# A fused two-block model on one core: front and both ends of the recurrence rebuilt, one inverse turned on VectorE, modulation products spread out

## What is computed

```python
m_lat = silu(c) @ mod_w + mod_b          # six rows of 1024; the same for c_ctx
h_ctx = rmsnorm(ctx, norm1_pre) * (1 + m_ctx[1]) + m_ctx[0]     # 256 tokens
h     = rmsnorm(x, norm1_pre) * (1 + m_lat[1]) + m_lat[0]       # 512 tokens
cols  = h @ w_in                         # hyena, rwkv and gate columns
kk = heads(k * k_k); kk = kk * rsqrt(max(sum(kk * kk), 1e-24))  # 8 heads of 64
for each of two directions:              # recurrence over 256 + 512 tokens
    S = S * w_t + (S @ a_t) b_t + v_t k_t ;  y = S @ r_t
y = head_groupnorm(y_0 + y_1) * ln_g + ln_b + bonus ;  y = y * (sigmoid(lg) @ g_up)
```

## Time and profile before

| | us |
|---|---|
| median of 3 runs (4183.6 to 4188.72) | 4186.31 |
| the profiled execution's own time | 4191.89 |
| its span | 4190.1 |
| PE busy | 3504.0 (84%) |
| VectorE busy | 1176.1 (28%) |
| ScalarE busy | 608.9 (15%) |
| mean DMA rate | 159 GB/s |

### The profile page before, as it was taken

The page is one execution under the profiler, slowest core; times in us unless marked ns, Lnnn a source line. Parts: engine busy times, 40 slices in busy tenths (PEclk is TensorE's granted clock), DMA queues, the critical chain, the costliest instruction groups (busy, mean ns, idle before and its releaser), DMA issues. The chain is left out here.

```text
span 4190.1 us, 50871 instructions
## 1 busy us (share of the span) xinstructions
PE 3504.0 (84%) x22440; PEld 1717.7 (41%) x22440; DVE 1176.1 (28%) x1979; ACT 608.9 (15%) x1182; POOL 7.9 (0%) x36
## 2 busy tenths in 40 slices
PE   3777899766989787777777789998999995999999
PEld 1446787632433432222222224345444443444443
DVE  0244556533200400000000002475366304122210
ACT  0113223111000210000000002215211102121100
POOL 0000000000000000000000000000000000000000
PEclk7888999877999699999999999999999996999999
DMA  9023322301012139999999971110243325312211
GB/s 334 21 66 124 123 84 89 80 30 64 31 60 75 42 158 421 422 420 421 422 418 421 421 311 44 61 51 16 71 148 116 113 71 155 106 60 80 80 66 50
DMA packets 227200, 664.82 MB, mean 159 GB/s; under 512 B 36960, under 2 KB 101156, under 8 KB 176293
## 3 DMA queue, kind: packets, MB, share of 16 engines
q1 hardware_dynamic: 225224, 661.02, 41.5%
q10 hardware_dynamic: 1757, 0.56, 0.1%
HBM read 638.84 MB, written 20.21 MB: 157 GB/s over the span
## 5 line engine op out<-in xcount | busy, mean ns | idle before, releaser
L2386 PE MATMUL banks<-h_T,weight_ring 128*128 128x512 f32 x1408 | 614.3, 597 | 5.8 <-PEq L89 5.8
L1820 PE MATMUL banks<-weight_ring,xe_T 128*64 128x512 f32 x2048 | 470.4, 602 | 150.1 <-DMA weight_ring<-in_exp_w 148.0
L2386 PEld LDWEIGHTS banks<-h_T,weight_ring 128*128 128x128 f32 x1408 | 268.0, 192 | 338.8 <-issue 338.7
L1820 PEld LDWEIGHTS banks<-weight_ring,xe_T 128*64 128x64 f32 x2048 | 143.2, 137 | 466.8 <-issue 260.0
L1600 PE MATMUL banks<-weight_ring,ffn_act 128*128 128x512 f32 x704 | 307.3, 600 | 14.5 <-PEq L2536 7.5
L1835 PE MATMUL banks<-weight_ring,hid_T 128*64 128x512 f32 x1024 | 235.3, 602 | 83.4 <-DMA weight_ring<-in_exp_w 82.5
L2445 DVE SCALAR_TENSOR_TENSOR conv<-banks,cols,conv 128x510 f32<-128x510 f32 (+1 forms) x176 | 131.9, 749 | 342.5 <-ACT conv L2415 337.8
L1600 PEld LDWEIGHTS banks<-weight_ring,ffn_act 128*128 128x128 f32 x704 | 135.4, 193 | 186.4 <-issue 186.4
L1889 DVE TENSOR_TENSOR hid<-silu,banks 128x1024 f32<-128x1024 f32 x16 | 19.5, 1221 | 665.8 <-issue 570.7
L549 PE MATMUL banks<-h_T,weight_ring 128*128 128x512 f32 x416 | 180.5, 592 | 3.2 <-PEq L89 3.2
L1835 PEld LDWEIGHTS banks<-weight_ring,hid_T 128*64 128x64 f32 x1024 | 71.4, 137 | 246.6 <-issue 142.2
(11 more groups left out here) (541 smaller groups left out, 3929.5 us busy)
## 6 DMA issues: line engine op xcount, KB each, us to landing
weight_ring<-in_exp_w SPq DMA_DIRECT2D x192, 2048.0 KB, 11.2
weight_ring<-in_ada_w SPq DMA_DIRECT2D x24, 2048.0 KB, 10.3
weight_ring<-in_ffn_w_up SPq DMA_DIRECT2D x44, 1024.0 KB, 7.5
weight_ring<-in_mod_w SPq DMA_DIRECT2D x12, 2048.0 KB, 9.0
weight_ring<-in_ffn_w_down SPq DMA_DIRECT2D x10, 2048.0 KB, 7.8
weight_ring<-in_attn_w_in SPq DMA_DIRECT2D x7, 2048.0 KB, 7.8
weight_ring<-in_w_in SPq DMA_DIRECT2D x6, 2048.0 KB, 9.8
weight_ring<-in_w_in SPq DMA_DIRECT2D x9, 1024.0 KB, 7.8
```

What stands on the lines that cost most here:

```text
L1820: mm = pe.matmul(k.ps[64 * half:64 * half + 64, 2 * c + b % 2, :], xeT[:, kt, e * CAP:(e + 1) * CAP], w[:, r, 512 * b:512 * b + 512], star ...
L2386: mm = pe.matmul(k.ps[:, b + c, :], w[:, c, kt, m * P:m * P + P], hT[:, kt, :], start=kt == 0, stop=kt == 7)
```

## The change

Only the first block's mixer and the order of its weights change.

- `modulation` and `small_columns` go. `front` does the first four chunks of mod_w (shift and scale of the first norm) and the norms of context and x in one stage. The partial sums are added and turned by four matmuls of two columns (`modulation_columns`), with no transfers. x is issued behind the ring's first three chunks, context at the stage's start. h of the 512 tokens is stored to DRAM.
- Chunks 4 to 7 of mod_w go into `rwkv_prepare`, 8 to 11 into `rwkv_finish`.
- `rwkv_prepare` gathers the lengths of all 8 heads on 8 partitions (headsel), has one root, one maximum and one reciprocal of 8x768, and spreads them again by matmuls (pick). `rwkv_finish` does the same with 8x512. It works on four tiles side by side.
- In the scan T is no longer carried by a product of its own: VectorE turns TT into T in 32x32 blocks (the last level, which couples blocks of 32, needs no T). Two of a round's four modulation products stand between the chain's halves, one each behind levels 1 and 3.
- The reload of x and the second `normed_columns` go: h and x are loaded during `rwkv_finish`.

```diff
-    out += [[rows(I["mod_w"][0], 0, 8, 512 * j, 512)] for j in range(12)]
+    out += [[rows(I["mod_w"][0], 0, 8, 512 * j, 512)] for j in range(FRONT_MODS)]
     out += [[rows(w_in, 0, 8, HY_COLS + 512 * j, min(512, RW_COLS - 512 * j))] for j in range(4)]
+    out += [[rows(I["mod_w"][0], 0, 8, 512 * j, 512)] for j in range(FRONT_MODS, FRONT_MODS + LATE_A)]
...
-            sync.dma_start(k.x[:], I["x"][0].rearrange("(t p) n -> p t n", p=P)).then_inc(consts_landed, 16)
             k.ring.load_ahead(sync, 0)
+            sync.dma_start(k.x[:], I["x"][0].rearrange("(t p) n -> p t n", p=P)).then_inc(k.rows_landed, 16)
...
+def modulation_columns(pe, k, part, bank, col0, n):
+
+    for m in range(4):
+        mm = pe.matmul(k.ps[:, bank, col0 + n * m:col0 + n * m + n], part[:, m * P:m * P + P], k.misc[:, 7:7 + n],
+                       start=True, stop=True)
+    return mm
```

The front's TensorE and ScalarE programs:

```diff
+            for j in range(n_chunks):
+                k.ring.wait(pe, j)
+                modulation_product(pe, k, j, j).then_inc(products, 1)
+                if j:
+                    turn_columns(j - 1)
+            turn_columns(n_chunks - 1)
+            pe.wait_ge(normed, tiles)
+            for j in range(DT):
+                a, b = pairs[j % 4]
+                if j == 3:
+                    pe.wait_ge(factors, 1)
+                if j >= 4:
+                    pe.wait_ge(evac_a, j - 3)
+                    pe.wait_ge(evac_v, j - 3)
...
+            for j in range(n_chunks - 1):
+                copy(j)
+            act.wait_ge(k.rows_landed, 32)
+            for u in range(tiles):
+                if u:
+                    act.wait_ge(squares, u)
+                act.activation(sqr[:], source(u), ACT.Square, accum_out=ss[:, 0, u:u + 1]).then_inc(squares, 1)
```

rwkv_prepare and the scan:

```diff
+            product(0)
+            product(1)
+            pe.wait_ge(loads, 96)
+            for j in range(RW_T):
+                pe.wait_ge(squared, j + 1)
+                pe.matmul(k.ps[0:2 * RW_T, 0, :], B.headsel[:, j, :], sqr[:, j % 2, 0:L], start=j == 0, stop=j == RW_T - 1)
...
-                pe.wait_ge(act_done, act_n[("siga", n, 1)])
-                for m in range(4):
-                    k.ring.wait(pe, 4 * n + m)
-                    ev(("mod", 4 * n + m), M.products(pe, k, 4 * n + m, (6, 7, 2, 5)[m]))
+                else:
+                    early_products(0)
...
                         products(("X", n, l, d), n, d, 3 * d + 1, "T", "Y")
-                        if l < LEVELS - 1:
-                            products(("XT", n, l, d), n, d, 3 * d + 2, "Y", "T")
+                    if l % 2:
+                        modulate(4 * n + 2 + l // 2)
...
-                    ev(("T1", n, d), dve.tensor_tensor(masks("T", d), masks("L", d), mask(d, "pair"), ALU.mult))
-                    after(("T1", n, d))
-                    ev(("T", n, d), dve.tensor_tensor(masks("T", d), masks("T", d), eye8, ALU.add))
...
+                    after(("TT", n, d))
+                    ev(("T", n, d), dve.transpose(flat("T", d), flat("TT", d)))
...
+    doubling = (("TTl", 0, 0), ("Tl", 0, 0), ("TTl", 0, 1), ("Y", 1, 0), ("Tl", 0, 1), ("Y", 1, 1))
```

rwkv_finish (SyncE, and the order on TensorE):

```diff
+            sync.dma_start(gup, k.I["rw_g_up"][0]).then_inc(gate_landed, 16)
+            sync.dma_start(k.hT[:], k.h_rows).then_inc(k.h_stored, 16)
+            sync.dma_start(k.x[:], k.I["x"][0].rearrange("(t p) n -> p t n", p=P)).then_inc(k.rows_landed, 16)
+            k.ring.load_ahead(sync, LATE_B)
...
+    pe_n = counted([("mean", 0), ("mean", 1), ("bonus", 0), ("bonus", 1), ("mean", 2), ("mean", 3)] + [("head", j) for j in last] +
+                   [("bonus", 2), ("bonus", 3), ("mod", 0), ("mod", 1), ("gate", 0), ("gate", 1), ("mod", 2), ("share", 0), ("share", 1),
+                    ("mod", 3), ("share", 2), ("gate", 2), ("share", 3), ("gate", 3), "columns"])
```

More of the change, by code:

```diff
@@ L413, in _ @@
             def _(pe):
[L414 to L417, removed]
+                for q in range(4):
+                    mm = pe.matmul(k.ps[:, 0, 0:self.rows], self.tiles[:, q, :], k.sq("eye")[0:self.rows, 0:self.rows],
+                                   start=q == 0, stop=q == 3)
                 mm.then_inc(turned, 1)
@@ L422, in _ @@
                 dve.wait_ge(turned, 1)
[L423 to L452, removed]
-                    if j >= M.n_buf:
-                        act.wait_ge(spread[j % M.n_buf], 64 * M.n * (j // M.n_buf))
-                    act.activation(M.part[:, j % M.n_buf, :], k.ps[:, j % 4, :], ACT.Copy).then_inc(copied, 1)
-                    act.wait_ge(copied, j + 1)
-                    for dma in M.spread(act, j, j % M.n_buf):
-                        dma.then_inc(spread[j % M.n_buf], 16)
-                for b in range(M.n_buf):
-                    act.wait_ge(spread[b], 64 * M.n * (n_chunks // M.n_buf))
-        k.ring.done(n_chunks)
-        M.finish(k, out, bias_name, bias0)
@@ L480, in _, with copy @@
         @block.scalar
         def _(act):
[L482 to L492 removed]
+            def copy(j):
+                act.wait_ge(products, j + 1)
+                act.sem_inc(k.ring.used, 1)
+                act.activation(part[:, j, :], k.ps[:, j, :], ACT.Copy).then_inc(copied, 1)
@@ L847, in _, with copy, values @@
-            act.activation(B.lwla[0:64, :], B.lwla[0:64, :], ACT.Tanh)
-            act.activation(B.lg[:], B.lg[:], ACT.Sigmoid)
-            for c in range(TOK // P):
+            def copy(m):
+                act.wait_ge(products, m + 1)
+                act.sem_inc(k.ring.used, 1)
+                act.activation(part[:, m, :], k.ps[:, 6 + m % 2, :], ACT.Copy).then_inc(copied, 1)
+            def values(c):
                 act.wait_ge(turned, c + 1)
@@ L1024, in chain, with modulate, early_products @@
                         ev(("y", n, i), mm)
+                    if i == 0 and not last:
+                        early_products(n + 1)
+            def modulate(m):
+                k.ring.wait(pe, m)
+                ev(("mod", m), M.products(pe, k, m, MOD_BANK[m % 4]))
+            def early_products(n):
+                pe.wait_ge(act_done, act_n[("siga", n, 1)])
+                for m in range(2):
+                    modulate(4 * n + m)
             def products(name, n, d, bank, left, right):
@@ L1395 @@
+    k.ring.done(LATE_B)
 class RwkvBuffers:
```

554 lines of the change are left out of this document (338 added, 216 removed).

## The result

The changed kernel takes **4007.8 us** (median of 4 runs, 4003.3 to 4015.8) against 4187.3 us before (4 runs): ratio 0.9575, 95% interval 0.9558 to 0.9591. That is 180 us less; 224 were predicted, and 4007.8 lies 2.8 us outside the range. The profiled execution took 4006.8 us with a span of 4005.0, so 185 us less than the 4190.1 of before. (The medians give 5 us less: the profiled execution of before took 4191.9, 4.6 above its median.)

The account below looks back on a forecast made before the run. Outside the projection, PE was taken to wait in the stages ahead of the untouched 3294 us, whose savings reach the end one for one; -83 - 9 - 83 - 49 = -224, against the median 4186.3 gives 3962 us, range 3932 to 4005.

Parts of the forecast that it names:

- Front (-83): Stages ahead of the first projection: four chunks instead of twelve, no spreads; projection starts at 59.5 instead of 142.4, -83 us.
- Transposition (t = 0.69): VectorE's transposition of 128x512 in the scan, taken at 0.69 us like a tensor-tensor of the same size.
- the transposition is dear: Rival, chance 0.13: the scan's VectorE transpositions cost more; 3995 at 1.24 us each, 4102 at 3.35.
- the estimate of 1.24 us: Scan transposition of 512 columns, priced as four times the skill page's 311 ns; +33 us on the sum.
- Scan (-83): Scan rounds: inverse starts 11.3 us earlier and takes 2.8 less, one latent round -14.1, sum -83 us.
- in two of the four level changes a modulation product of 1.79 stands ahead of the next Y: Scan's inverse: 1.55 of each product shows, so levels of 4.2 and 5.75 us, 19.9 for 22.7.
- Behind the scan (-49): rwkv_finish and the stage after it: 26 us go whole, the rest by four tiles together; -49 us, ends -30 and -52.
- the gain's store and the barriers: the next projection at about 846.5: End of the stage behind the scan: VectorE's last column at 842, next projection at about 846.5.
- what would make it wrong: Wrong if inverse levels wait for chunks, PE's clock falls there, or reloading h and x delays chunks behind the scan.
- rwkv_prepare (-9): rwkv_prepare and the Silu stage: scan starts at 305.5 instead of 314.6, -9 us, ends -11 and +13.
- columns 1.2, two shares 2.8: End of PE's chain in rwkv_prepare at full clock: columns 1.2 us, last two shares 2.8, to 302.7.
- Half clock in the moved products: Rival, chance 0.12: rwkv_prepare and the stage behind the scan keep the low clock, +22 and +19, 4003.

Follow-up runs that it names:

- e7: Changed kernel with a second, idle transposition of the same size ahead of each of the 60 in the scan; 4025.4 us.
- e4: Changed kernel with the two chunks per round that the level products set free cut to their first eighth, part of the loading left out; 3987.9 us.
- e3: Changed kernel with the two chunks that the level products set free issued only behind the inverse; 4002.8 us.
- e5: Changed kernel with the level products' chunks loaded in four pieces of 512 KB, each gated by a later event; 3990.6 us.
- e11: Changed kernel with the level products' chunks loaded in two pieces of 1 MB; 3994.6 us.
- e8: e1 with the recurrence's projection loading two chunks ahead, the third issued in rwkv_prepare behind the small loads; 3995.7 us.
- e1: Changed kernel with the six gain stores moved from rwkv_finish to the head of the hyena projection's stage; 3998.0 us.
- e2: Changed kernel with five of the gain stores issued at the head of rwkv_finish, ahead of its loads; 4023.2 us.

## Why the prediction missed by 40 us

- **Front (-83): right.** Measured -83.9, with the first projection product at 58.5 where 59.5 was worked out. The steps came out as well: the root at 43.2 for 43.4, the last normed tile at 47.7 for 47.9.
- **Transposition (t = 0.69): right,** 0.706 to 0.711; levels 4.2 us, and 10.14 for the two of which one holds a product. The rival "the transposition is dear" is out, and with it the estimate of 1.24 us. Its slope was too steep besides: in e7 0.7 us more for each cost 0.29, not 0.7.
- **Scan (-83): the chain was right, and a cost was missing.** The step that failed is "in two of the four level changes a modulation product of 1.79 stands ahead of the next Y", which costed the moved product alone. The product also brings its DMA: the 2 MB transfer that it triggers now runs beside the densest instruction stretches of the program (16 records of a modulation product take 1.8 us, 32 of the inverse 0.94), and PE stops there for want of instructions. Before, the transfers ran beside the modulation products and L and stopped PE for 8.9 us; now it is 17.3, and the pair of levels with one product takes 12.12 us for 9.95 in round 3. With that transfer shrunk, the scan is 409.3 us for a forecast of 409.8. Round 3, which had only 0.7 us of stops before, gains 14.0 for 14.1; that the whole comes so close is in part luck, for e4 also lacks 6.6 us of the stops that the forecast kept. That the transfer's burst causes the stops is shown by e3, e4, e5 and e11. That it does so by delaying instructions is shown by the packets of the instruction queue, late in the burst, with every stop ending just behind one. How the two share the DMA engines, and why PE needs another 2.4 to 2.7 us, no run shows.
- **Behind the scan (-49): mis-sized by 15 us.** The step is "the gain's store and the barriers: the next projection at about 846.5", which gave a few us for the end. PE's and VectorE's work was as reckoned (VectorE's last column 36.3 us behind the turn of the modulation; forecast 34.6, 842 less 807.4). The six stores of 4-byte elements behind three chunks took 25.6 us of SyncE's time. With them elsewhere the tail is 38.7 (e8) to 42.7 us (e1), for 39.1 forecast. The "what would make it wrong" clause looked at the reload of h and x, which held up nothing: the fourth chunk was late by 0.79 us.
- **rwkv_prepare (-9): mis-sized by 6 us.** The step is "columns 1.2, two shares 2.8" with the full clock assumed for them. The columns took 4.2 us, the last two shares 5.5 and the two turns before them 3.3 for 1.9: 7 us more, at a granted clock of 0.63. The 3.6 us wait for the small loads was not reckoned either, but it cost nothing against the forecast, because the first two products took 3.6 us where 7.2 were put: the head sums ended 12.4 us into the stage, for 12.8. e8 shows the same from the other side: its wait is 0.3, its first two products take 5.3, and the stage is only 2.0 us shorter.
- **Half clock in the moved products**: the mean granted clock rose from 0.62 to 0.84 and from 0.60 to 0.76 in these stages, so the rival did not come as priced (+22 and +19). It came in part, in the last 13 us of rwkv_prepare. That its time (4003) was near is chance.
- **The range** took in each rival alone. What happened was two unforeseen collisions in the DMA system at once, in the two stages that lack 37 us together, in a kernel whose steps were all costed on PE, ACT and VectorE.

## What to carry to other kernels

When an instruction that frees a buffer is moved, move its transfer along in your mind: ask what runs beside that burst. A large prefetch does not only compete for bytes; cut into pieces of 0.5 to 1 MB that are gated by progress, it cost this PE-dense loop 4 to 5 us where whole chunks cost 17.

A stage that ends in a barrier ends with its last issue too: look at the queue ahead of the final stores, and put stores of 4-byte elements where neither a load nor a barrier stands behind them.

## What the runs showed of the hardware

- PE's instructions come in packets of 16 KB, one for every 254 to 257 records (82 in the scan of the changed kernel, 93 before). Where a packet came late beside a 2 MB transfer (8.6 us behind the last one in round 3, where e4 has 3.9 to 5.6), PE stopped; in the four pairs of stops 255 matmul records apart it stood for 1.5 to 2.3 us each time. It went on 2.4 to 2.7 us behind the packet, in all 48 stops of before, the changed kernel, e3, e4, e5 and e11.
- A store of 1024 elements of 4 bytes took about 2.5 to 3 us of all DMA engines (after, e1, e2), and five of them held the next issue for 15.6 us (e2). The issue of one such store took 0.4 us with nothing ahead of it, and 8.8 us behind five others.
- STREAM_TRANSPOSE of 128x512 in fp32 costs VectorE what a tensor-tensor of that size does, 0.71 us against 0.69.
